# A two-block transformer kernel: the part ahead of the experts rebuilt, and half of the expert queries moved between the expert slots

## What is computed

```python
def first_block(x, ...):
    h = rms_norm(x, norm1_g)
    y = h @ w_in                      # q 512, k 128, v 128, p 512 columns
    a = swa_attention(q, k, v, q_norm_g, k_norm_g, attn_sinks, rel_bias)
    b = pool_mixer(p, pool_w, pool_scale)
    x = x + concatenate([a, b]) @ w_out
    h2 = rms_norm(x, norm2_g)
    return x + peer(h2, peer_wq, peer_subkeys, peer_u, peer_v)

def peer(h, wq, subkeys, u_tab, v_tab):          # 8 heads, top 16 of 128 keys, twice
    q = (h @ wq).reshape(T, 8, 2, 128)
    sc = einsum('thpd,hpnd->thpn', q, subkeys)
    v1, i1 = top_k(sc[:, :, 0], 16); v2, i2 = top_k(sc[:, :, 1], 16)
    best, pos = top_k(v1[..., :, None] + v2[..., None, :], 16)
    experts = e1 * 128 + e2                      # 16384 experts, 128 of them a token
    gates = softmax(best)
    u, vv = u_tab[experts], v_tab[experts]       # 4 KB each a token and expert
    return einsum('tk,tkd->td', gates * gelu(einsum('tkd,td->tk', u, h)), vv)
```

## Time and profile before

| | us |
|---|---|
| median of 3 runs (1346.12 to 1347.58) | 1346.55 |
| the profiled execution | 1346.53 |
| its span | 1344.7 |
| TensorE busy (81% of the span) | 1083.5 |
| VectorE busy (60%) | 804.8 |
| GpSimd busy (55%) | 734.1 |
| ScalarE busy (34%) | 457.5 |

### The profile page before, as it was taken

One profiled execution on the slowest core, in us unless ns is written; L12 is line 12 of the kernel. 1 busy time (PEld: TensorE's weight loads), 2 busy tenths in 40 slices (PEclk: granted clock), 3 DMA queues, 4 the chain that ended last, 5 costly groups with the idle time before them and its releaser, 6 DMA issues.

```text
span 1344.7 us, 14972 instructions
## 1 busy us (share of the span) xinstructions
PE 1083.5 (81%) x5004; PEld 739.4 (55%) x5004; DVE 804.8 (60%) x1519; ACT 457.5 (34%) x961; POOL 734.1 (55%) x446
## 2 busy tenths in 40 slices
PE   4278898768777777777777777799989999799997
PEld 3267784223222222223222232499878998789996
DVE  4073456677576675858667555433233848779777
ACT  3135543211212112121121212344646533544442
POOL 2334574464344443544435334089567886588884
PEclk9579998999999999999999999899999999799999
DMA  7522376999999999999999999445335454455552
GB/s 233 120 98 78 121 295 247 423 421 420 422 421 421 422 421 422 421 421 420 422 422 405 413 417 418 172 164 173 121 123 173 134 169 153 141 188 190 186 188 94
DMA packets 66825, 373.60 MB, mean 278 GB/s; under 512 B 7465, under 2 KB 9737, under 8 KB 33673
## 3 DMA queue, kind: packets, MB, share of 16 engines
q0 software_dynamic: 36864, 268.45, 48.3%
q1 hardware_dynamic: 25920, 94.38, 21.1%
q10 hardware_dynamic: 3976, 9.93, 2.8%
HBM read 369.59 MB, written 2.62 MB: 277 GB/s over the span
## 4 chain that ended last, share of the span: by engine, by line
PE 41%; DMA 34%; DVE 14%; ACT 5%; POOL 3%; issue 3%; ACTq 0%; DVEq 0%; SPq 0%; POOLq 0%
DMA arena<-in_peer_uv,idx_all 30%; PE ps L1115 10%; PE ps L1116 10%; PE ps L1117 10%; PE ps L1299 8%; DVE arena L951 4%; DMA rel_scratch<-arena 2%; POOL w_hl L309 2%; POOL arena L323 1%; ACT prob L521 1%; DVE yT L1088 1%; PE ps L1327 1%; DVE arena L1086 1%; ACT xT L380 1%; DVE xT L695 1%
## 5 line engine op out<-in xcount | busy, mean ns | idle before, releaser
L1299 PE MATMUL ps<-arena,prob 128*128 128x512 f32 x1024 | 487.4, 622 | 161.4 <-ACT prob L521 161.2
L309 POOL TENSOR_TENSOR w_hl<-ring,w_hl 128x1024 fp32r<-128x1024 f32 x178 | 447.0, 2520 | 233.1 <-ACT w_hl L373 232.0
L323 POOL DMA_INDIRECT arena<-in_peer_uv,idx_all x256 | 285.5, 1115 | 361.6 <-PE ps L1299 341.0
L1299 PEld LDWEIGHTS ps<-arena,prob 128*128 128x128 f32 x1024 | 190.9, 196 | 456.8 <-ACT prob L521 260.0
L951 DVE CUSTOM_DVE_ANT_0 arena<-arena,xn 128x1024 f32<-128x1024 f32 x256 | 318.7, 1245 | 181.8 <-DMA arena<-in_peer_uv,idx_all 179.0
L1115 PE MATMUL ps<-xT,w_hl 128*128 128x256 f32 x864 | 248.6, 288 | 10.9 <-DVE xT L695 4.3
L1116 PE MATMUL ps<-xT,w_hl 128*128 128x256 f32 x864 | 246.1, 285 | 0.0
L1117 PE MATMUL ps<-xT,w_hl 128*128 128x256 f32 x864 | 246.0, 285 | 0.0
L373 ACT ACTIVATE w_hl<-ring 128x1024 fp32r<-128x1024 f32 x178 | 186.9, 1055 | 170.5 <-PE ps L1117 121.2
L1115 PEld LDWEIGHTS ps<-xT,w_hl 128*128 128x128 f32 x864 | 167.4, 194 | 14.3 <-issue 8.0
L516 ACT ACTIVATE gel<-acts 128x2 f32<-128x2 f32 x128 | 26.0, 203 | 431.8 <-DVE acts L951 431.8
(11 more groups left out here) (210 smaller groups left out, 982.0 us busy)
## 6 DMA issues: line engine op xcount, KB each, us to landing
ring<-in_weights SPq DMA_DIRECT2D x178, 512.0 KB, 3.3
arena<-in_peer_uv,idx_all POOLq DMA_INDIRECT x256, 13.1
arena<-in_rg_weights ACTq DMA_DIRECT2D x1, 2048.0 KB, 7.6
rel_scratch<-arena ACTq DMA_DIRECT2D x1, 1536.0 KB
x<-in_x SPq DMA_DIRECT2D x2, 512.0 KB, 5.3
arena<-in_subkeys ACTq DMA_DIRECT2D x1, 1024.0 KB, 13.7
bias<-rel_scratch ACTq DMA_DIRECT2D x1, 1024.0 KB, 5.6
out_x<-x ACTq DMA_DIRECT2D x2, 512.0 KB, 2.6
```

The source lines that it names most:

```text
L309: pool.tensor_tensor(w_hl[:, n % SPLIT, 1, :], ring[:, n % RING, :], w_hl[:, n % SPLIT, 0, :].bitcast(F32), ALU.subtract).then_inc(w_lo, 1)
L323: pool.indirect_dma_start(uv_ring[:, n % GRING, :], None, A["peer_uv"], bass.IndirectOffsetOnAxis(idx_all[:, h, c:c + 1], 0))\
L1299: j = pe.matmul(banks(2 + 2 * t + half), diag[:, n % GRING, :], uv_ring[:, n % GRING, D + half * 512:D + (half + 1) * 512], start=(h == 0 ...
```

## The change

1. The bias table. `rel_scratch` shrinks to 8 rows of `REL_N` (12 KB), is stored by SyncE once, and is loaded back by SyncE with overlapping reads of it (the one-hot is reversed, and VectorE reads the bias backwards). SyncE waits for VectorE's copy of the table and for its own store. The loads of `inv_cnt`, `pool_w`, `norm2_g` and `subkeys` move from ScalarE's queue at the start to SyncE's, behind weights 6, 10 and 12.
2. VectorE starts with the two first softplus operations and the table's copy, then x's square. ScalarE's first work after the roots is one split and the first tile of `evac_xT`. The rest of softplus (26 small operations) stands behind the second norm.
3. The gains of q and k are applied by ScalarE in the evacuation of their transposes.
4. Scale, bias and maxima come ahead of the pool evacuations, tile by tile.
5. v is stored twice side by side (`v1`), and `values` multiplies it by the transposed probabilities, so that the output is born transposed; `o_sb` and its transposes go. It runs in two parts around the probability transposes. The last four output weights go tile by tile.
6. Addition, norm and transposes of tile 0 come before tile 1's.
7. `topk_stage` takes a list of tiles. Head 0's runs for tile 0 before the slots and for tile 1 in slots 0 to 8; head 1's in slots 9 to 25.
8. Only eight queries (`QUERIES_FIRST`) come before the slots. The others stand between slots, one every six (`SLOTS_PER_QUERY`), with their splits: `SPLIT_FIRST` is 29, and GpSimd makes the low parts of 29 to 36 behind gathers 8, 14, ... 50.

The rest of the diff is the same operations under new names, and higher semaphore counts in the second block.

```diff
-        rel_dram = nc.dram_tensor("rel_scratch", (HEADS, P, REL_N), F32).ap()
+        rel_dram = nc.dram_tensor("rel_scratch", (HEADS, REL_N), F32).ap()
...
+            sp_.dma_start(sinks[:], A["sinks"].broadcast_to([P, HEADS])).then_inc(sinks_ld, 16)
+            sp_.wait_ge(rel_cp, 1)
+            sp_.dma_start(rel_dram, rel_tab[0:HEADS, :]).then_inc(rel_st, 16)
+            sp_.wait_ge(rel_st, 16)
+            sp_.dma_start(bias[:], bass.AP(tensor=rel_dram.tensor, offset=1,
+                                           ap=[[1, P], [REL_N, HEADS], [1, SEQ]])).then_inc(bias_ld, 16)
+            for n in range(RING, 4 * RING):
+                next_weight(n)
+                if n == 6:
+                    sp_.dma_start(inv_cnt.rearrange("p a b -> p (a b)"),
+                                  A["inv_cnt"].broadcast_to([P, 4 * SEQ])).then_inc(pool_ld, 16)
+                    sp_.dma_start(pool_w[:], A["pool_w"]).then_inc(pool_ld, 16)
+                if n == 10:
+                    sp_.dma_start(row_gain[:], A["norm2_g"].broadcast_to([P, D])).then_inc(row_ld, 16)
+                if n == 12:
+                    sp_.dma_start(subk[:], A["subkeys"]).then_inc(subk_ld, 16)
...
-                pool.wait_ge(tk, (h + 1) * TOPK_STAGES)
                 for c in range(SLOTS):
+                    if c == 0 or (h == 0 and c == TOPK):
+                        pool.wait_ge(tk, topk_at(h, c // TOPK) + TOPK_STAGES)
                     gather(h, c)
-                    n = SPLIT_FIRST + c - 1
-                    if h == 0 and SPLIT_FIRST <= n < W_X2:
-                        split_lo(n)
-                    if h == 1 and c % 4 == 0 and c < 4 * AHEAD:
-                        split_lo(W_X2 + c // 4)
+                    late = (h * SLOTS + c - GRING) / SLOTS_PER_QUERY
+                    if late in range(W_X2 - SPLIT_FIRST + AHEAD):
+                        split_lo(SPLIT_FIRST + int(late))
...
-            for n in range(3):
-                split_hi(n)
             act.wait_ge(cols_ld, 16)
-            act.wait_ge(spx, 2)
-            act.activation(sp[:, 1, :], sp[:, 0, :], ACT.Exp).then_inc(spa, 1)
-            for t in range(NT):
-                evac_xT(0, t, C_N1)
-            act.wait_ge(rel_mm, 1)
-            act.copy(rel_tab[0:HEADS, :], banks(7)[0:HEADS, 0:REL_N]).then_inc(rel_cp, 1)
-            act.wait_ge(rel_cp, 1)
-            act.dma_start(rel_dram, bc(rel_tab[0:HEADS, :], 1, P)).then_inc(rel_st, 16)
-            act.wait_ge(rel_st, 16)
-            act.dma_start(bias[:], bass.AP(tensor=rel_dram.tensor, offset=P - 1,
-                                           ap=[[REL_N - 1, P], [P * REL_N, HEADS], [1, SEQ]])).then_inc(bias_ld, 16)
-            for n in range(3, W_P + AHEAD):
+            split_hi(0)
+            evac_xT(0, 0, C_N1)
+            split_hi(1)
+            evac_xT(0, 1, C_N1)
...
+            def heads_out(t, kv):
+                n = 2 * t + kv
+                act.wait_ge(pv_done, n + 1)
+                src = banks((2, 3, 0, 1)[n]).rearrange("p (c r n) -> p c r n", c=2, r=2)
+                for r in range(2):
+                    rows = slice(r * HD, (r + 1) * HD)
+                    i = act.activation(yT[rows, 0, 2 * kv:2 * kv + 2, t * P:(t + 1) * P], src[rows, :, r, :],
+                                       ACT.Identity)
+                i.then_inc(aT_done, 1)
...
+            for m in range(QUERIES_FIRST):
+                split_hi(W_PQ + m + AHEAD)
+                query(m)
+                if m % 2 == 0 and m:
+                    scores_out(m // 2 - 1)
+                if m == 5:
+                    gate_exps(0, range(0, 1))
+            scores_out(QUERIES_FIRST // 2 - 1)
             for h in range(PH):
                 for p in range(SLOTS // 2):
                     pair_weights(h, p)
+                    late, step = divmod(2 * (h * SLOTS // 2 + p), SLOTS_PER_QUERY)
+                    m = QUERIES_FIRST + late
+                    if step == 0 and m < 2 * PH:
+                        split_hi(W_PQ + m + AHEAD)
+                    if step == SLOTS_PER_QUERY - 2 and m <= 2 * PH:
+                        if m < 2 * PH:
+                            query(m)
+                        if late and m % 2 == 0:
+                            scores_out(m // 2 - 1)
+                    if h == 0 and p == 3:
+                        gate_exps(0, range(1, 2))
                     if h < PH - 1 and p == 11:
...
+            dve.wait_ge(rel_mm, 1)
+            dve.tensor_copy(rel_tab[0:HEADS, :], banks(7)[0:HEADS, 0:REL_N]).then_inc(rel_cp, 1)
...
+            def mix_add(t):
+                dve.tensor_tensor(x[:, t, :], x[:, t, :], banks(4 + 2 * t, 2), ALU.add).then_inc(mix_added, 1)
+            dve.wait_ge(sums_done, 1)
+            mix_add(0)
+            dve.wait_ge(row_ld, 16)
+            rstd(1, 0)
+            normalised(0, with_gain=True)
             dve.wait_ge(w_used, W_OUT + 8)
-            for t in range(NT):
-                dve.tensor_tensor(x[:, t, :], x[:, t, :], banks(4 + 2 * t, 2), ALU.add).then_inc(mix_added, 1)
-            dve.wait_ge(row_ld, 16)
-            for t in range(NT):
-                rstd(1, t)
-                normalised(t, with_gain=True)
+            mix_add(1)
+            rstd(1, 1)
+            normalised(1, with_gain=True)
             for t in range(NT):
                 evac_xT(1, t, None)
-            LANES = [(r, r // 2, r % 2) for r in range(4)]
-            def topk_stage(h, stage):
+            softplus()
...
+            def topk_steps(h, c):
+                if h == 0 and c <= TOPK_STAGES // 2:
+                    for stage in range(2 * c, min(2 * c + 2, TOPK_STAGES)):
+                        topk_stage(0, stage, (1,))
+                elif h < PH - 1:
+                    stage = c if h else c - TOPK_STAGES // 2 - 1
+                    if stage < TOPK_STAGES:
+                        topk_stage(h + 1, stage)
...
+            def values(t, kv):
+                for kt in range(t + 1):
+                    g = GROUPS.index((t, kt, kv))
+                    i = pe.matmul(banks((2, 3, 0, 1)[2 * t + kv]), v1[:, kt, kv].rearrange("p a d -> p (a d)"),
+                                  prob_group(0, g), start=kt == 0, stop=kt == t)
                 i.then_inc(pv_done, 1)
-            for t in range(NT):
-                pe.wait_ge(o_evac, t + 1)
-                for c in range(4):
-                    i = pe.transpose(banks(t)[:, c * P:(c + 1) * P], o_sb[:, t, c * P:(c + 1) * P], ident[:])
-                i.then_inc(oT_done, 1)
-            pe.wait_ge(aT_lo, 2)
-            for c in range(4):
-                row_product(W_OUT + 4 + c, lambda t: parts(yT, c, slice(t * P, (t + 1) * P)), False, c == 3)
+            prob_transposes(0, range(0, 2))
+            for kv in range(KV):
+                values(0, kv)
+            prob_transposes(0, range(2, 6))
+            for kv in range(KV):
+                values(1, kv)
+            def heads_ready(c, t):
+                pe.wait_ge(aT_lo, 2 * t + c // 2 + 1)
+            row_products_by_tile([(W_OUT + 4 + c, c) for c in range(4)], rows_of_yT, heads_ready)
...
+                    late, step = divmod(n, SLOTS_PER_QUERY)
+                    m = QUERIES_FIRST + late
+                    if step == 1 and m <= 2 * PH:
+                        if late:
+                            key_scores(m - 1)
+                        if m < 2 * PH:
+                            query_product(m)
```

More of the change, by code:

```diff
@@ L419, in _ @@
             for t in range(NT):
-                act.copy(v1[:, t, :], banks(6 + t)[:, P:2 * P]).then_inc(v1_done, 1)
-            act.wait_ge(qkms, 2)
-            act.activation(qk_root[:], qk_ss[:], ACT.Sqrt).then_inc(qkroot, 1)
+                for half in range(2):
+                    i = act.copy(v1[:, t, :, half, :],
+                                 banks(6 + t)[:, P:2 * P].rearrange("p (k d) -> p k d", d=HD))
+                i.then_inc(v1_done, 1)
+            act.wait_ge(qkms, 1)
+            act.activation(qk_root[:], qk_ss[:], ACT.Sqrt, bias=eps_col[:], scale=1.0 / HD).then_inc(qkroot, 1)
             for g in range(4):
@@ new lines, in probabilities @@
+            def probabilities(b, t):
+                dve.wait_ge(exp_done, 2 * b + t + 1)
+                if b == 0:
+                    dve.tensor_tensor(den[:, t, :], den[:, t, :], esink[:, t, :], ALU.add).then_inc(den_step, 1)
+                    dve.wait_ge(den_step, 2 * t + 1)
+                dve.reciprocal(rden[:, t, :], den[:, t, :]).then_inc(den_step, 1)
+                dve.wait_ge(den_step, 2 * t + 2 if b == 0 else 4 + t + 1)
+                dve.tensor_tensor(prob_view(t), prob_view(t), bc(rden[:, t, :], 2, P * (t + 1)),
+                                  ALU.mult).then_inc(p_done, 1)
@@ L834, in _ @@
             dve.wait_ge(const_ready, 7)
+            dve.wait_ge(sinks_ld, 16)
+            for t in range(NT):
+                scores_in(0, t, HD ** -0.5, lambda off: bias[:, :, SEQ - 1 - off::-1])
+                maxima(0, t)
```

(39 more changed lines are left out.)

407 lines of the change are left out of this document (181 added, 226 removed).

## The result

The changed kernel takes 1297.43 us (median of 4 runs, 1295.69 to 1300.57) against 1346.34 for the kernel before in the same session: a ratio of 0.9637, 95% interval 0.9619 to 0.9655. The forecast was 1293 us with a range of 1279 to 1312. The spans differ by 1344.7 - 1298.8 = 45.9 us, the medians by 48.9.

A forecast was written before the change was run, and what follows sets the result against it. Transfers were taken to pace the expert part at 2.50 us a slot, with the 32.57 us rel_scratch store stalling TensorE ahead of it. Terms summed to 53.7 us: 1346.5 - 53.7 = 1293 us, range 1279 to 1312.

The forecast's parts named there:

- (a): Start up to the first q product: now at 21.00, expected at 18.0, a gain of 3.0 us (2 to 5).
- (b): First q product to last pool product, with the rel_scratch store's stall: 30.8 in place of 59.45, gain 28.6 us (27 to 31).
- (c): Last pool product to first output product, now 22.9 us: VectorE's new order takes 18.2, gain 3.6 us (1 to 5).
- (d): Attention output, now 24.1 us: fewer narrow matmuls, copies and transposes make it near 19.6, gain 4.5 us (3 to 6).
- (e): Norm, now 8.8 us: the first tile's part goes under the second tile's products, leaving 7.4; gain 1.4 us (0.5 to 2.5).
- (f): First query to first gather, now 27.0 us: GpSimd's splits still hold the gathers, a table load adds a little; -0.4 us (-1.5 to 0).
- (g): Start of the experts: queries between slots let TensorE take slots at once, avoiding lost transfer time; gain 13 us (3 to 18).
- the stall stays: Rival: the small store is slow for a cause other than its 1.5 MB; stall gain about 3, 1319 us, chance 0.03.
- held TensorE: Rival, expert slots: the ring doesn't absorb a query's 3.4 us, eight times 27 us; 1320 us, chance 0.07.
- the slower one: Rival, expert slots: the ring drains at every query, 11.5 us each, eight times 92; 1385 us, chance 0.03.
- Locked VectorE: Rival, expert slots: each of eight splits between slots costs VectorE its 2.4 us in full, 19 together; 1312 us, chance 0.05.
- TensorE at half clock in the first slots: Sign that the forecast is wrong: TensorE at half clock in the first 48 expert slots.

The follow-up runs named there:

- e4: The changed kernel with splits 12 and 13 moved from under VectorE's pooling steps to behind the exponentials: 1295.15 us, ratio 0.9626 to the kernel before.
- e2: The changed kernel with softplus moved behind head 0's top-k and the first tile's gates: 1295.29 us, ratio 0.9615 to the kernel before.
- e5: e2 with the first eight gathers issued ahead of GpSimd's splits 27 and 28: 1292.81 us, ratio 0.9602 to the kernel before.
- e9: e8 with head 0's top-k run for both tiles together before the slots: 1295.51 us, ratio 0.9634 to the kernel before.
- e3: The changed kernel with all sixteen queries ahead of the slots, splits 29 to 33 behind the first gathers: 1302.19 us, ratio 0.9661 to the kernel before.
- e8: e5 plus e4's edit, with head 0's key scores taken right behind the second query: 1289.8 us, ratio 0.958 to the kernel before.
- e10: e8 with GpSimd's split 26 also behind the first eight gathers: 1289.06 us, ratio 0.9586 to the kernel before.

## Why the prediction was right, and where its steps were off

By stage, between the profiled executions:

| term | forecast | measured | places after |
|---|---|---|---|
| (a) first q product | 3.0 | 2.3 | 18.69 |
| (b) the stall | 28.6 | 28.4 | 18.69 to 49.49 |
| (c) to the first output product | 3.6 | 1.1 | 49.49 to 71.59 |
| (d) attention output | 4.5 | 2.3 | 84.42 to 106.2 |
| (e) norm | 1.4 | 1.5 | 106.2 to 113.50 |
| (f) first query to first gather | -0.4 | -4.5 | 113.50 to 145.0 |
| (g) first to last gather | 13 | 13.7 | 145.0 to 795.1 |
| elsewhere | 0 | 1.1 | pool half of the output, and behind the last gather |
| sum | 53.7 | 45.9 | |

The forecast is 4.4 us from the measured median; most of its steps were too good by a little, and one by more.

(a), (b) and (e) held, with their mechanisms. The copy took 0.55, the chain was late as said, and SyncE's wait had its cover: the table load was issued at 11.86 and weight 4 at 15.06.

(c) is a term mis-sized. The forecast knew that GpSimd can hold the pooling and took half of one split; there were two, split 13 and the tail of the four before it, (3.01 - 1.27) + (4.23 - 2.21) = 3.8 us by the rows of after, and e4. e4 shows that about 1.7 of it can be had back.

(d) is a term mis-sized too. The forecast let the second tile's values be "partly under" the four groups of probabilities. They stand behind them in TensorE's list: 84.42 to 94.66 are 10.2 us where I had 8.4. The groups themselves were quicker than said, 3.5 us in place of 4.2. This is read from the two traces alone; no experiment separates it.

(f) is the step that failed. It gave softplus for nothing, because VectorE was idle for 9.7 us and the operations need 5.3. It priced each at its time alone and named the idle gap as cover, but not what runs beside it: GpSimd's splits. With six operations held, softplus lasted 18.0 us, and e2 shows it gone. Of the 4.1 us by which the term missed, softplus is 2.8 or 2.9 (e2). The other 1.3 are the first query, which the forecast ran at full clock and which found it at half (0.50 where the kernel before had 1.00); that is read from the traces alone, no run changes it by itself. Splits 27 and 28 ahead of the gathers were in the forecast, and e2 and e5 show them: once softplus is away, they are next. The remark that the top-k of one tile "brings nothing by itself" was true of this order alone; where nothing else stands ahead of the gathers, e9 prices it at about 6 us.

(g) came out at its size, in part by luck, since the reason was half right. The DMA did fill at once and no query drained the ring. But (f) and (g) aren't independent: with the queries first, the ring opens at their end, so a late first gather costs nothing and shrinks the loss. With the first gather where the changed kernel has it, queries first cost 5.7 us (e3), not the 15 to 17 that I had put on them. Together (f) and (g) were to bring 12.6 and brought 9.2. The same view says what the change left unused: 31.5 us from the first query to the first gather, which e8 cuts to 22.5.

The rivals: the stall stays, held TensorE and the slower one didn't come. Locked VectorE did, but elsewhere: in the slots the ring absorbed it; in the pooling, where VectorE is the chain, it cost 3.7 us (e4 gets 1.7 of them back and gives the rest to the split's next victim), and 2.9 of the 12.7 us that softplus was held reached the first gather (e2). I had looked for the lock where a dot product had shown it, and not where small operations would meet it.

Of the signs named, two of the wrong ones came: TensorE at half clock in the first slots (0.54), and GpSimd waiting for indices at the first gather, as much as for splits. The first output product (71.6, not 68), the end of the output products (106.2, not 101) and the first gather (145.0, not 136) were late. One sum is wrong: the high bounds of the terms add up to 67.5 and not to 65.5, so 1279 is their corner itself and holds nothing for overlaps; the result lies far inside either way.

## What to carry to other kernels

Cost a small operation that is moved into an idle gap by what runs on the other engines in that gap, not by its time alone: here 5 us of work became 18 beside splits that it had never met. When a saturated stage follows, first find from which event its end is counted (here the first gather, or the end of the queries), since only what moves that event counts, and an edit's worth changes with it. And before an edit is priced from one place in two traces, compare the granted clock there: in e2 it hid 1.3 us of 2.9.

## What the runs showed of the hardware

A VectorE operation of 8 elements a partition can last as long as a whole GpSimd split of 1024: 2.25 us in place of 0.17, for two inputs (L763) and for one input and a constant (L768). Searches were not held: beside the split of 126.15 in e2, two MAX8 took 0.49 us together and each FIND_INDEX8 0.28 or 0.29, as elsewhere, while a CAST at 128.84, beside the next split, took 2.40 in place of 0.18. The Trainium skill (SBUF — State Buffer, Who interferes with whom) says that `copy`, `cast` and `tensor_scalar` can contend with GpSimd in their 2-port modes, and two-input operations with its reads. By that rule, the trace agrees.

Where splits follow each other, a waiting VectorE instruction doesn't always get in between. The dot was 3.43 us long beside one, 5.41 beside two (e8, 144.16) and 8.41 beside three (e10), and each time ended about 1.1 us after the last of them. But the softplus operation of 114.55 ended at 116.80, between the two splits of 114.40 (4.75 us for both). What decides it, no run here shows. And the hold goes both ways. In e4 a division of VectorE began 0.26 us ahead of a split, and the split took 4.29 us in place of 2.40:

```profile
71.11 2.29 DVE L847 TENSOR_TENSOR prob<-prob,rden 128x2048 f32<-128x2048 f32 x1
...
71.37 4.29 POOL L336 TENSOR_TENSOR w_hl<-ring,w_hl 128x1024 fp32r<-128x1024 f32 x1 [5.60 <-ACT w_hl L393]
```

The old store ran at a small part of what the queues can do. The kernel before, by stretch, and the line of all packets of the DMA view of the same 20 us:

```profile
30.00:50.00 20.00, 1.60 (x8) 0.98 (x6) 0.00 (x0) 0.00 (x0) 0.00 (x0) 0.65 0.45 51
...
DMA packets 667, 1.02 MB, mean 51 GB/s; under 512 B 0, under 2 KB 667, under 8 KB 667
```

51 GB/s at a DMA share of 0.45, against 419 at 1.01 for the gathers. Its outermost dimension had 8 rows. The Trainium skill (DMA: Bandwidth & Descriptors, Rules for kernel authors) says that such a size under 16 confines a DMA to at most that many of the 16 engines; a share under one half agrees with it. That can't be all of it: at a full share the store would have moved 51 / 0.45 = 113 GB/s, and the gathers moved 419 / 1.01 = 415. Its packets were of 1.5 KB, the gathers' of 7.3 (268.45 MB in 36864). No run here tried the old store in another shape, so how much of the 28.7 us its shape would have given back stays open.
